# The routing of all blocks at once with the norm on VectorE, and an even attention with spread turns, unit 0 ahead and the head norm's factors in the output weights

## The chip, the cores and the metric

The kernel runs on one core of a Trainium2 chip. The metric is the device time of one execution in microseconds (us). Engines: TensorE (PE, its weight loads PEld), VectorE (DVE), ScalarE (ACT), GpSimd (POOL), SyncE (SP, which issues most DMAs).

## The reference, cut to what matters

Two transformer stages follow each other on 512 tokens of width 1024, all in float32. The second has two layers, an even and an odd one, and each ends in a routed mixture of 32 experts. What the change touches:

```python
# even layer: differential attention, 4 heads of 2 maps; then a norm over each head
a_out = rmsnorm(softmax(q1 k1) v - lam * softmax(q2 k2) v, subln_g) * (1 - lambda_init)
m = concatenate([a_out, latent_attention]) @ w_o       # w_o: 1024 x 1024
# both layers: norm, then the router
x = layer_norm(ALPHA * x + m, ln1_g, ln1_b)
grp = argmax(softmax(x @ w_rg + b_rg))                 # 4 groups of 8 experts
top_v, top_i = top_k(e_logits of that group, 2)
gate = softmax(top_v) * g_w
# experts: each token's two rows, gathered in lists per expert
y = silu(xb @ w1[e]) * (xb @ w3[e]) @ w2[e] * w
```

## The kernel before

A stage is a class whose methods write one instruction list per engine; the order on each engine is the order written out, and engines wait for each other on counting semaphores (`wait_ge`). `then` issues an operation and makes its own engine wait for its end. `wait_end` waits for all that an earlier stage has signalled.

**Products (`Dense`).** A product goes through pieces of 128 rows of a weight matrix. For each piece ACT makes a rounded high part (L692) and DVE the rest (L727, or L729 when the weights are scaled by a gain). PE then multiplies three times for each of four token blocks (L189, the helper `mm`), and DVE or ACT take the accumulators out. `pe_beside(i)`, `act_beside(i)` and `dve_beside(i)` insert other work after piece i.

**`EvenProj`** (38 pieces) makes queries, keys and values of the even layer. Pieces 32 and 33 are followed by the turns of head 0.

**`EvenMix`** has 32 units of 128 query rows: units 0 to 15 are the 4 differential heads (two score maps each), 16 to 31 the 8 latent heads, two at a time. In step n PE turns the weights of unit n-3 (L2436), makes the scores of unit n (L2420 or L189), does one turn of heads where `due` has one (L2400) and multiplies the values of unit n-5 (L2452 or L2457). DVE takes each map's maximum (L2549), the reciprocals of the sums (L2558, L2566), and combines the maps of even units (L2611). POOL combines those of odd units (L2641, L2642) and divides later ones (L2654). ACT does the exponentials (L2506). A turned head goes to PSUM bank 7; ACT takes the high half (L2488), then DVE the low half (L2541, L2544), and only then may PE use the bank for the next. `due` puts k and q of heads 1 to 3 in steps 1, 2, 5, 6, 9 and 10, then the latent heads (mk, mq) in steps 11 to 26 without a gap, and the mixed heads in 28 to 31. Steps 26 and 27 of `dve_norm` multiply the four normed heads by the row factor and by the gain, block by block (L2589, eight operations a step).

**`OutRoute`** (two layers) is the output product, the norm, the router and the lists. In its last four pieces (`pe_blocks`, `dve_blocks`) the work goes block by block: PE finishes a block's sum, DVE adds it to x (L772), takes the statistics (L3123, L3124), ACT the root (L3068), DVE the reciprocal. PE turns the block (L3036) and makes its 36 logits from the raw rows. The norm of block 0 is two DVE operations (L3150, L3145). Blocks 1 to 3 are scaled by ACT (L3074), then POOL multiplies by the gain (L3252) and adds the bias (L3253). Each normed block is written to `xd` and `xa` by SP. Then `route` corrects the logits with the statistics (L3175, L3177, pair by pair for four blocks), finds the group with `top8` over padded values (L3156, L3159, L3161), masks, finds the experts with `top8`, makes one-hots (L3195, their sum L3197), and the gates. `lists` copies the two PE sums from PSUM, adds the prefixes block by block, makes ranks, and builds selectors by eight comparisons (L3230). PE multiplies the selectors with token numbers and gates (L189 on 64 columns), and four operations make the row numbers (L3237 to L3240). POOL gathers the tokens of experts 0 and 1 (L3261). SP loads the weights of expert 1 only after the first gather, those of expert 0 earlier.

**`Experts`** turns the gathered tokens (L3343), splits the weights (L3408, L3463) and multiplies, expert after expert, with the weights streaming in.

## Time and profile before

| | us |
|---|---|
| median of 3 runs | 3568.32 (3567.33 to 3570.15) |
| the profiled execution | 3554.19 |
| its span | 3552.9 |
| even attention | 129.4, from 1744.0 to 1873.4 |
| blocks and routing, first layer | 49.3, from 1911.4 to 1960.7 |
| experts, first layer | 603.2 |

The profile is one execution. PEclk is the granted clock of TensorE as a share of 2.4 GHz. Idle time of an engine is put down to who released it; the chain is followed back from the last instruction.

### The profile page before, as it was taken

The page shows a single profiled execution, that of the slowest core. Times are in us where ns is not written, and L with a number is a line of the kernel's source. Part 1 is how long each engine was busy: PE and PEld are TensorE (multiplying, and loading weights), DVE is VectorE, ACT ScalarE, POOL GpSimd, SP SyncE. Part 2 cuts the span into 40 slices and gives each one's busy share as a digit, 9 for nine tenths or more (in the row PEclk, how much of TensorE's full clock was granted, in tenths as well). Part 3 has the DMA queues.
Part 4 walks back from the last instruction along what each step waited for, and adds up shares of the span by engine and source line. Part 5 has one row for each costly group of instructions (what it writes and reads, how often), then busy time and mean ns, then how long its engine had stood idle before and what let it go on. Part 6 is the DMA issues. An engine that isn't in the chain of part 4 may idle for free. (4 is left out here: it accounts for less than half of the span.)

```text
span 3552.9 us, 42265 instructions
## 1 busy us (share of the span) xinstructions
PE 3270.6 (92%) x16668; PEld 2719.4 (77%) x16669; DVE 2241.1 (63%) x3508; ACT 1801.9 (51%) x2689; POOL 394.9 (11%) x331
## 2 busy tenths in 40 slices
PE   8989899999989999999987999999789879999995
PEld 6789777877878777878766777788667868888874
DVE  5755343435855443333675888899743668988886
ACT  3333342323333342333462778888633628888884
POOL 1101000000101000000141111111100121111110
PEclk9988999999989999999998999999989989999998
DMA  4210122221120122222203899988722238898994
GB/s 139 72 56 1 64 79 95 95 81 63 50 80 1 48 95 75 93 88 89 72 1 110 327 351 364 359 348 353 301 71 103 80 144 336 357 361 356 361 359 178
DMA packets 135163, 590.99 MB, mean 166 GB/s; under 512 B 29616, under 2 KB 35632, under 8 KB 110256
## 3 DMA queue, kind: packets, MB, share of 16 engines
q1 hardware_dynamic: 115664, 569.92, 41.5%
q0 software_dynamic: 19296, 18.30, 2.2%
q8 instruction: 135, 2.21, 0.2%
q14 instruction: 68, 0.56, 0.0%
HBM read 594.40 MB, written 44.04 MB: 180 GB/s over the span
## 5 line engine op out<-in xcount | busy, mean ns | idle before, releaser
L189 PE MATMUL ps<-r,r 128*128 128x512 f32 (+4 forms) x11048 | 2593.7, 393 | 66.8 <-DVE r L2075 23.1
L189 PEld LDWEIGHTS ps<-r,r 128*128 128x128 f32 x11048 | 2046.2, 190 | 536.8 <-issue 63.8
L3463 DVE TENSOR_TENSOR r<-mem,r 128x1024 fp32r<-128x1024 f32 x768 | 902.5, 1220 | 133.6 <-ACT r L3408 127.3
L3408 ACT ACTIVATE r<-mem 128x1024 fp32r<-128x1024 f32 x768 | 788.3, 1061 | 226.5 <-PE ps L189 144.4
L692 ACT ACTIVATE r<-mem 128x512 fp32r<-128x512 f32 (+3 forms) x518 | 338.7, 661 | 906.4 <-PE ps L189 900.0
L727 DVE TENSOR_TENSOR r<-mem,r 128x512 fp32r<-128x512 f32 (+1 forms) x272 | 185.5, 688 | 436.6 <-ACT r L692 435.5
L729 DVE SCALAR_TENSOR_TENSOR r<-mem,r 128x512 fp32r<-128x512 f32 (+3 forms) x246 | 171.7, 714 | 263.6 <-ACT r L692 261.9
L3321 POOL DMA_INDIRECT xa<-mem,memu x64 | 101.5, 1587 | 964.7 <-ACT mem L3433 964.7
L3261 POOL DMA_INDIRECT mem<-xd,memu x64 | 99.2, 1550 | 84.2 <-PE ps L3343 35.1
L1666 PE MATMUL ps<-mem 128*128 128x65 f32 x800 | 99.8, 282 | 0.0
L1666 PEld LDWEIGHTS ps<-mem 128*128 128x128 f32 x800 | 96.7, 199 | 0.0
L1874 DVE RECIPROCAL mem<-ps 128x4 f32<-128x4 f32 x40 | 7.3, 182 | 132.8 <-PE ps L1666 132.7
L1792 ACT ACTIVATE mem<-ps 128x512 f32<-128x512 f32 (+1 forms) x96 | 46.6, 525 | 87.3 <-PE ps L1654 87.0
L3433 ACT ACTIVATE mem<-ps,mem 128x512 f32<-128x512 f32 x128 | 80.7, 686 | 13.0 <-PE ps L189 13.0
L3469 DVE TENSOR_TENSOR r<-ps,r 128x512 fp32r<-128x512 f32 x128 | 82.1, 681 | 4.4 <-ACT r L3413 4.4
L537 PE MATMUL ps<-mem 128*128 128x128 f32 x288 | 44.4, 306 | 43.6 <-DVE mem L3696 19.7
L3343 PEld LDWEIGHTS ps<-mem 128*128 128x128 f32 x512 | 68.1, 192 | 18.0 <-issue 12.9
L3343 PE MATMUL ps<-mem 128*128 128x128 f32 x512 | 69.0, 279 | 12.6 <-DMA mem<-xd,memu 12.6
L3413 ACT ACTIVATE r<-ps 128x512 fp32r<-128x512 f32 x128 | 68.6, 586 | 17.2 <-PE ps L3343 17.2
L537 PEld LDWEIGHTS ps<-mem 128*128 128x128 f32 x288 | 36.7, 157 | 51.7 <-issue 28.2
L189 PE MATMUL ps<-mem 128*128 128x93 f32 (+3 forms) x320 | 50.3, 324 | 25.5 <-DMA mem<-in_nsa_cmp_w 14.7
L1861 DVE TENSOR_REDUCE mem<-ps 128x1 f32<-128x512 f32 (+3 forms) x160 | 67.4, 480 | 6.7 <-PE ps L1624 6.4
(392 smaller groups left out, 2883.2 us busy)
## 6 DMA issues: line engine op xcount, KB each, us to landing
mem<-in_w_up SPq DMA_DIRECT2D x80, 2048.0 KB, 18.5
mem<-in_w_down SPq DMA_DIRECT2D x80, 2048.0 KB, 7.9
mem<-in_w_gate SPq DMA_DIRECT2D x64, 2048.0 KB, 13.2
mem<-in_w_in SPq DMA_DIRECT2D x10, 2048.0 KB, 7.9
mem<-in_odd_w_qkv SPq DMA_DIRECT2D x6, 2048.0 KB, 8.4
mem<-in_w_o SPq DMA_DIRECT2D x4, 2048.0 KB, 10.4
mem<-in_rel SPq DMA_DIRECT2D x16, 512.0 KB, 3.3
mem<-in_even_w_in SPq DMA_DIRECT2D x3, 2048.0 KB, 8.0
```

The lines of the kernel that those rows point to most:

```text
L189: r = e.matmul(out, a, b, start=start and i == 0, stop=stop and i == n - 1, skip_group_check=skip)
L537: r = pe.e.transpose(self.ps(u)[:, k, :], src[:, c:c + 128], self.K.ident)
L692: act.e.activation(wh, w, ACT.Copy, scale=scale).then_inc(*self.S["dn_hi"](self.p0 + i))
L727: r = dve.e.tensor_tensor(wl, w, wh.bitcast(F32), SUB)
L729: r = dve.e.scalar_tensor_tensor(wl, w, job.gain[:, kk:kk + 1], wh.bitcast(F32), MUL, SUB)
L1666: r = pe.e.matmul(self.result(n)[:, 65 * t:65 * t + 65], src[:, c:c + 128], self.F.V[:, j, slot, :], start=j == 0, stop=j == t)
L3261: pool.e.indirect_dma_start(self.XG[e % 2], None, self.K.xd[:, :], bass.IndirectOffsetOnAxis(self.IDX[:, 1, e:e + 1], 0), bounds_check=S - ...
L3321: pool.e.indirect_dma_start(self.K.xa[:, :], bass.IndirectOffsetOnAxis(self.R.IDX[:, 1, e:e + 1], 0), self.YY[e % 2], None, bounds_check=S ...
L3343: r = pe.e.transpose(self.turned(half)[:, k, :], self.XG[e % 2][:, 4 * half + k::8], self.K.ident)
L3408: act.e.activation(wh, w, ACT.Copy).then_inc(*self.S["ex_wh"](self.l, e, i))
L3463: dve.e.tensor_tensor(wl, w, wh.bitcast(F32), SUB).then_inc(*self.S["ex_wl"](self.l, e, i))
L3469: dve.e.tensor_tensor(self.XL[e % 2][:, k, :], self.turned(half), self.XH[e % 2][:, k, :].bitcast(F32), SUB).then_inc(*self.S["ex_xl"](sel ...
```

## The change

In `EvenProj`, unit 0's scores follow piece 35, and its maxima and exponentials follow on DVE and ACT. `EvenMix` starts its loops for these at unit 1. The buffers of E are rotated so that unit 0's lie outside the projection's weight ring. `due` places mk and mq of the eight latent heads in steps 3, 11, 14, 17, 20, 22, 24 and 26 and the ones after them; each head has one of four buffers. The head norm's gain goes into the output weights (`gain=source.M.sg`, four columns of the gain and four of ones), and the norm is one operation a head. In `OutRoute` DVE does the norm of all four blocks (`norm`), ACT and POOL none; the logits are corrected as they come. The group is found by a maximum, a comparison and the smallest index over all blocks. PE adds the rank prefixes in the accumulator; the selectors are two operations and in the single-pass type; POOL makes the values (numbers, and the gates in a high and a low part).

```diff
 class OutRoute
+    def norm(t):
+            x = K.X[:, t, :]
+            dve.wait_ge("rt_p", self.l, "turn", t, 1)
+            dve.then("ln_g", v.scalar_tensor_tensor(x, x, self.nmu[:, t:t + 1], self.gains.gb, ADD, MUL), sid, t)
+            v.scalar_tensor_tensor(x, x, self.mv[:, t, 1:2], self.gains.bb, MUL, ADD).then_inc(*S["ln_b"](sid, t))
...
         for t in range(4):
+            if t:
+                norm(t - 1)
+            if t == 3:
+                self.logits(dve, 0)
...
             job.dves(dve, self, job, t, self.acc(job, t)[:, 0:job.n])
             moments(t)
             roots(t)
+        self.logits(dve, 1)
+        norm(3)
...
-        for t in range(1, 4):
-            x = K.X[:, t, :]
-            pool.wait_ge("ln_a", sid, t)
-            pool.then("ln_g", pool.e.tensor_tensor(x, x, self.gains.gb, MUL), sid, t)
-            pool.then("ln_b", pool.e.tensor_tensor(x, x, self.gains.bb, ADD), sid, t)
+        pool.wait_ge("rt_v", l, "oh")
+        p.tensor_tensor(OV[:, :, :, 0:32], self.oh, bc(self.val.rearrange("p t k -> p k t"), 3, 32), MUL)
+        pool.wait_ge("rt_v", l, "gt")
+        pool.then("rt_g", p.tensor_tensor(self.gates, self.oh, bc(self.gt.rearrange("p t k -> p k t"), 3, 32), MUL))
+        pool.then("rt_g", p.tensor_copy(OV[:, :, :, 32:64], self.gates))
+        p.tensor_tensor(OV[:, :, :, 64:96], self.gates, OV[:, :, :, 32:64].bitcast(F32), SUB).then_inc(*S["rt_g"](l, "values"))
...
 pe_blocks
-                if i == n - 3:
-                    if j >= 1:
-                        self.pe_turn(pe, j - 1)
-                    if j >= 2:
-                        self.pe_logits(pe, j - 2)
+                if i == n - 3 and j >= 1:
+                    self.pe_turn(pe, j - 1)
+                if i == n - 2 and j >= 2:
+                    self.pe_logits(pe, j - 2)
+        self.pe_logits(pe, 2)
         self.pe_turn(pe, 3)
-        self.pe_logits(pe, 2)
         self.pe_logits(pe, 3)
...
 route
+        dve.then("rt_v", v.tensor_reduce(self.gm, groups, AX.X, MAX))
+        v.tensor_tensor(goh, groups, bc(self.gm, 2, 4), ALU.is_equal).then_inc(*S["rt_v"](l, "goh"))
+        v.tensor_tensor(ge, groups, bc(self.gm, 2, 4), SUB).then_inc(*S["rt_v"](l, "ge"))
+        dve.then("rt_v", v.tensor_tensor(goh, goh, bc(self.first, 1, 4), MUL))
+        dve.then("rt_v", v.tensor_reduce(self.mn, goh, AX.X, MIN))
+        dve.then("rt_v", v.tensor_tensor(goh, goh, bc(self.mn, 2, 4), ALU.is_equal))
+        dve.then("rt_v", v.tensor_scalar(goh, goh, 1.0, 1e30, SUB, MUL))
+        dve.then("rt_v", v.tensor_tensor(ml.rearrange("p t (g n) -> p t g n", g=4),
+                                         lg[:, :, 4:36].rearrange("p t (g n) -> p t g n", g=4), bc(goh, 3, 8), ADD))
...
+        dve.then("rt_v", v.tensor_tensor(oh, bc(bc(ei, 1, 4), 1, 2), bc(which, 3, 32), ALU.is_equal), l, "oh")
...
 lists
+        dve.then("rt_v", v.tensor_tensor(self.ranked, self.oh, bc(ranks, 1, 2), MUL))
+        dve.then("rt_v", v.tensor_reduce(self.rv.rearrange("p t k -> p k t"), self.ranked, AX.X, ADD))
         for k in range(2):
-            for t in range(4):
-                r = v.tensor_scalar(self.OS[:, k, t, :], self.iota, self.rv[:, t, k:k + 1], None, ALU.is_equal)
+            v.tensor_tensor(self.OS[:, k], bc(self.iota, 1, 4), bc(self.rv[:, :, k], 2, 128),
+                            ALU.is_equal).then_inc(*S["rt_v"](l, "os", k))
...
+        dve.then("rt_v", v.tensor_scalar(self.ixf, bank[1][:, 0:32], NONE, None, ADD))
+        v.tensor_copy(self.IDX[:, 1, :], self.ixf).then_inc(*S["rt_v"](l, "rows"))
...
 pe
+        pe.e.matmul(bank[:, 0:128], self.ustr, ohs, start=True, stop=False, skip_group_check=True)
+        for t in range(3):
+            o = bank[:, 32 * t + 32:128].rearrange("p (t n) -> p t n", n=32)
+            r = pe.e.matmul(o, self.ones, bc(ohs[:, 32 * t:32 * t + 32], 1, 3 - t), start=False, stop=t == 2,
+                            skip_group_check=True)
...
+        pe.wait_ge("rt_g", l, "values")
+        for k in range(2):
+            pe.wait_ge("rt_v", l, "os", k)
+            for t in range(4):
+                r = pe.e.matmul(K.bank[1][:, 0:96], self.OS[:, k, t, :], self.OV[:, k, t, :], start=k == 0 and t == 0,
+                                stop=k == 1 and t == 3)
...
 EvenProj
+        if i == 35:
+            self.mix.pe_scores(pe, 0)
...
+        if i == 36:
+            for m in range(2):
+                self.mix.act_exponentials(act, 0, m)
...
 EvenMix
-        for h in range(8):
+        for h, n in enumerate((3, 11, 14, 17, 20, 22, 24, 26)):
             for i, what in enumerate(("mk", "mq")):
-                self.due[11 + 2 * h + i] = (what, h)
+                self.due[n + i] = (what, h)
...
 dve_norm
-                for t in range(4):
-                    x = M.MIX[:, t, 128 * h:128 * h + 128]
-                    r = v.scalar_tensor_tensor(x, x, M.var[:, 4 * h + t:4 * h + t + 1], M.sg, MUL, MUL)
+                x = M.MIX[:, :, 128 * h:128 * h + 128]
+                v.tensor_tensor(x, x, bc(M.var[:, 4 * h:4 * h + 4], 2, 128), MUL).then_inc(*S["em_v"](sid, "mixed", h))
```

## Rows read from the trace of the kernel before

**Rows 1.** The page: lines of the chain that ended last, shares of the span.
```profile
PE ps L189 31%; DMA mem<-in_w_up 5%; PE ps L3343 1%; DMA mem<-in_w_gate 1%; ACT r L3408 1%; DVE r L3463 1%; PE ps L3384 1%; PE ps L2436 0%; DVE mem L2549 0%; DVE mem L3177 0%; ACT mem L3433 0%; DVE r L2863 0%; DVE r L2685 0%; PE ps L2457 0%; DMA xa<-mem,memu 0%
```
**Rows 2.** By stretch: us; PE, PEld, DVE, ACT, POOL busy (count); PEclk, DMA share, GB/s.
```profile
1744.00:1873.40 129.40, 111.11 (x842) 83.26 (x842) 91.72 (x193) 84.69 (x199) 55.07 (x52) 0.99 0.00 1
1764.00:1769.20 5.20, 5.20 (x35) 3.33 (x34) 3.78 (x9) 4.42 (x11) 1.95 (x3) 1.00 0.00 0
1775.40:1808.90 33.50, 28.66 (x193) 21.68 (x193) 22.81 (x47) 24.00 (x59) 16.09 (x16) 1.00 0.00 1
1911.40:1927.50 16.10, 15.32 (x100) 13.26 (x99) 10.12 (x26) 4.66 (x10) 2.56 (x2) 1.00 0.45 183
1927.50:1960.70 33.20, 8.52 (x54) 8.04 (x52) 27.14 (x95) 9.03 (x12) 15.38 (x7) 0.55 0.27 105
1960.70:2563.90 603.20, 589.75 (x2688) 479.63 (x2688) 521.00 (x508) 480.80 (x573) 95.15 (x62) 0.99 0.89 350
2888.00:2919.80 31.80, 7.87 (x51) 7.41 (x50) 26.67 (x93) 9.03 (x12) 14.90 (x7) 0.58 0.26 101
```
**Rows 3.** Timeline, blocks to experts: start, us, engine, line, operation [idle before it, releaser].
```profile
1913.86 1.28 DVE L3150 SCALAR_TENSOR_TENSOR mem<-mem 128x1024 f32<-128x1024 f32 x1
1915.10 0.69 DVE L772 SCALAR_TENSOR_TENSOR mem<-mem,ps 128x512 f32<-128x512 f32 x1
...
1925.98 0.69 DVE L772 SCALAR_TENSOR_TENSOR mem<-mem,ps 128x512 f32<-128x512 f32 x1 [2.97 <-PE ps L189]
...
1955.68 1.91 POOL L3261 DMA_INDIRECT mem<-xd,memu  x1 [15.73 <-DVE mem L3242]
...
1960.68 1.94 PE L3343 MATMUL ps<-mem 128*128 128x128 f32 x8 [6.81 <-DMA mem<-xd,memu]
```
**Rows 4.** DVE and POOL behind the blocks (first: one line's ns min/median/max).
```profile
L3177 DVE SCALAR_TENSOR_TENSOR mem<-mem x8: 255/2220/2373, 1929.9 to 2895.5; 128x36 f32<-128x36 f32 x8
...
1930.30 2.36 POOL L3252 TENSOR_TENSOR mem<-mem 128x1024 f32<-128x1024 f32 x1 [0.63 <-ACT mem L3074]
...
1930.34 2.37 DVE L3177 SCALAR_TENSOR_TENSOR mem<-mem 128x36 f32<-128x36 f32 x1
...
1938.87 1.11 DVE L3161 CAST mem<-memu 128x32 f32<-128x32 uint32 x1
```
**Rows 5.** Chain of waits in the routing: start, us, engine and line.
```profile
1942.30 0.76 DVE memu L3159 x5
...
1943.82 0.29 DVE r L3197
...
1948.49 1.67 DVE mem L3230 x8
1950.20 3.69 PE ps L189 x16
1953.91 0.20 DVE mem L3237
```
**Rows 6.** A line of POOL with 256 columns: ns min/median/max, first and last start.
```profile
L2000 POOL TENSOR_TENSOR mem<-mem x24: 717/732/742, 253.3 to 1187.8; 128x256 f32<-128x256 f32 x24
```
**Rows 7.** Timeline of the even attention, as rows 3.
```profile
1752.68 1.04 POOL L2641 TENSOR_TENSOR mem<-mem 128x512 f32<-128x512 f32 x1 [58.49 <-DVE mem L2559]
...
1784.71 0.64 PE L2400 MATMUL ps<-mem 128*96 128x128 f32 x4 [1.28 <-DVE r L2544]
...
1841.22 2.19 DVE L2589 SCALAR_TENSOR_TENSOR mem<-mem 128x128 f32<-128x128 f32 x8
...
1845.18 3.00 DVE L2589 SCALAR_TENSOR_TENSOR mem<-mem 128x128 f32<-128x128 f32 x8
...
1845.41 1.04 PE L2436 MATMUL ps<-mem 128*128 128x128 f32 x4 [3.04 <-DVE mem L2608]
...
1846.11 2.91 PE L189 MATMUL ps<-r,r 96*128 96x512 f32 x6
...
1851.26 1.63 PE L189 MATMUL ps<-r,r 96*128 96x512 f32 x6
```

More of the change, by code:

```diff
@@ L2299, in dve_beside @@
             v.tensor_copy(M.heads[0][1], K.bank[0][:, :]).then_inc(*S["em_lo"]("even_mix", "k", 0))
+        if i == 36:
+            for m in range(2):
+                self.mix.dve_maximum(dve, m)
     def pool(self, pool):
```

202 lines of the change are left out of this document (79 added, 123 removed).

## The prediction

> **What bounds the kernel now.** I read the page first. The chain that ended last runs mostly through the matmuls of TensorE (PE), with the weight stream of the experts behind it [rows 1]. So a microsecond counts only where PE waits. The busy times by stretch show where that is in the parts the change touches [rows 2]. The two passes over all 64 experts are PE and the weight stream side by side (589.8 of 603.2 us busy in the first). The attention of the even layer, 129.4 us, has PE busy for 111.1, so 18.3 us of it are waits. The blocks of the output product are full (15.3 of 16.1). What comes behind them is not: in 33.2 us of routing PE works 8.5 at a granted clock of 0.55, close to the lower of its two levels (1.2 of 2.4 GHz), while VectorE (DVE) is busy for 27.1. The second layer repeats that: 7.9 of 31.8. Both layers' routing is therefore a serial DVE chain with nothing of size beside it, and whatever leaves that chain leaves the time.
>
> **Routing, step by step (first layer; the second has the same rows 960.2 us later).** Before, the last block's accumulation starts on DVE at 1925.98, the gather is issued at 1955.68 and the first transposes of the experts start at 1960.68 [rows 3]. Six terms:
>
> (a) *Norm on DVE, from the last block to the logits.* Before, POOL multiplies and adds the gains of blocks 1 to 3 in six operations of 2.36 us. DVE's small operations of that stretch take as long as POOL's do: the logits operation of 128x36 takes 0.26 us at the least and 2.22 in the median of its eight, one of them beside POOL's from 1930.3 to its end at 1932.7, and a cast of 128x32 takes 1.11 [rows 4]. The change takes POOL out and gives DVE two passes of 1.28 us per block [rows 3]. I walked this through. Norm 0 now stands ahead of block 1's addition, which started at 1915.10 and now starts at 1916.4. PE's turn of block 1 waits 0.8 us for it. Norm 1 (2.6 us) ends as block 2's product does, which the wait and a postponed product have moved to 1921.3. Norm 2 ends as block 3's does, at about 1926.8, and logits 0 (0.46) are in front of block 3's addition, so it starts at 1926.9 instead of 1925.98. The statistics and the root then take the 2.3 us of before (the root is back by 1929.2), logits 1 0.5, norm 3 2.6, logits 2 and 3 0.9: logits complete at 1933.2. Before, they were complete at 1937.55, one end of POOL's after another (1932.7 and two times 2.4). Gain 4.4 us, of which PE's turn and logits of block 3 (about 1932.7) leave only half a microsecond unused. Bounds 3.1 (one more pass shows in front of an addition) and 5.3 (the shift of the last addition is avoided).
>
> (b) *Logits to the one-hots' sum.* Before 1937.58 to 1944.11, 6.5 us, of which POOL's last operation lengthened the cast by 0.9 [rows 4, 5]. After: two small reductions and five elementwise steps at 0.21, the masked add 0.32, eight values 0.5, their search 0.76, cast 0.22, both one-hots in one operation of 256 columns 0.46 (between the 0.29 of 128 and the 0.69 of 512), sum 0.29: 4.0 with the extra "ge" step [rows 3, 5]. (0.21 is the 0.20 of a small dependent step, rounded up.) Gain 2.5.
>
> (c) *Ranks.* Before, from 1944.11 to the ranks, just ahead of 1948.49, DVE copies PSUM, adds prefixes in six steps and multiplies and reduces twice, 4.35 us [rows 5]. After, PE adds the prefixes: four small matmuls at 0.3 each, 1.2 (the lists' sixteen ran at 0.23 [rows 5]), then one product (0.46) and one reduction (0.45), 2.2 with a wait. Gain 2.1. Bounds 1.4 (the matmuls at twice 0.23 and a hand-over) and 2.6.
>
> (d) *Lists' selectors.* Eight operations in 1.66 us become two of 128x512 at 0.69 (the size of the additions in [rows 3]), 1.35. But four POOL operations are new beside them: a 128x256 product takes POOL 0.73 us [rows 6], the last three wait for the gates, and [rows 4] show DVE held until POOL's end. I add two of them, 1.5 us. Loss 1.2, between a loss of 2.6 (all four) and a gain of 0.3 (none).
>
> (e) *Lists' matmuls.* Before, 16 instructions in 3.67 us, all behind the last selector [rows 5]. After, there are 8, four of which run while DVE builds the second half: four at 0.23 and a start, 1.0. Gain 2.7. Bounds 1.8 (all eight come behind the last selector) and 3.0.
>
> (f) *Indices.* Four dependent steps of 0.2 [rows 5] become two, gain 0.4. The gather's own 4.9 us and the 0.9 us in front of it stay.
>
> Sum 10.9 us a layer, 21.8 for two. Behind it nothing new is late: the token blocks for the gather leave DVE at 1932.4, so their writes are out by the time the gather wants them, about 1944.8; ScalarE and DVE split the first four weight pieces while the tokens are on their way, and both move together. The weights of expert 1 and later are issued after the first gather, so the stream starts earlier by the same amount.
>
> The skill bears on (d). The Trainium skill, "SBUF — State Buffer", section "Who interferes with whom", says that an operation of VectorE with two SBUF inputs and a GpSimd operation that reads SBUF exclude each other for a whole instruction. By this rule the trace agrees, 2.22 us against 0.26 on one form, and it speaks against the new POOL operations. Without the exclusion the layer's sum would be 12.4; with all four blocking, 10.9 less 1.4, that is 9.5.
>
> **The even attention.** Unit 0's scores, maxima and exponentials move into the projection, behind piece 35. They cost PE 1.1 us there, a unit's scores (a unit without a turn takes 2.6 with them), so the projection ends that much later; the copies that end it stay. DVE no longer has two maxima in front of its first sums. The first POOL combine, 1752.68 before, I place at 1751.9 [rows 7]: gain 0.8. Bounds 0 and 1.9.
>
> Turns: a unit that has a turn with a low half took 3.7 us from unit 11 to 19 (33.5 us for nine, PE busy 28.7), because DVE waits for ScalarE's high half, which waits for both exponentials; PE's wait of 1.28 us for DVE ahead of a turn is this alternation [rows 2, 7]. A unit without one takes 2.6 (two in 5.2, PE full). Three such units (13, 16, 19) lose their turn: -3.3. Units 3 and 4 gain one, +2.2 if they pay in full, and unit 27 gains one, +0.6. Net gain 0.5. Bounds: a loss of 2.8 (nothing comes back at 13, 16 and 19) and a gain of 3.3.
>
> Norm: 16 operations of 128x128, in two groups of 2.19 and 3.00 us, become four of 128x512 at 0.69, 1.4 a group [rows 7]. The first group stands on the chain: PE waits 3.04 us behind it, and then runs at its lower level (six matmuls 2.91 us, 1.63 five microseconds later). I take 0.9 for the first group and 1.3 for the second with part of the clock. Gain 2.2. Bounds 0.9 and 4.
>
> The part that the factors play in the output weights (ScalarE scales by a column, DVE's low part is a three-operand form) costs nothing: those pieces lie under the product, PE-bound; without that cover it would be 16 times 0.03.
>
> Sum 3.5. All: 21.8 + 3.5 = 25.3 us. The profiled execution took 3554.19 (span 3552.9), so it would take 3528.9; the median of the runs shown is 14.1 higher, and I take the same difference off it: **3543.0**.
>
> **Rivals.** A measurement of this kernel can tell about 0.2%, 7 us, from no change.
>
> *POOL's values set the lists* (0.13). Place: the wait "values" ahead of the lists' matmuls. POOL's three last steps start with the gates (about 1939.4) and take 0.73 each at least; a broadcast operand may cost more (the nearest other row is 1.04 for 512 columns). If DVE's two selectors also stand between them, values come 2 to 3 us behind my 1942.8. For it: [rows 4, 6]. Against: two of these four overlap DVE work that reads PSUM. Price 3 a layer: 3549.
>
> *The attention gives more* (0.12). PE waits 18.3 us there; if spreading breaks the ScalarE-DVE alternation also in the units that keep a turn, 8 more go: 3535. *It gives nothing* (0.12): units 3, 4 and 27 pay for their turns in full and nothing comes back: 0.8 and 2.2 won, 2.8 lost, 3546, and up to 3549 if the hoisted unit gains nothing either.
>
> *PE falls to its lower clock in the blocks* (0.02): the end on the other side. Place: turns 1 and 2 among the blocks, which now wait for DVE's additions behind the norms. The only fall in the attention followed a wait of 3.04 us [rows 7]; I forecast 0.8, and it decides only if waits of that length come up. Then the 15.3 us of PE work there [rows 2] double, in both layers: 30.6 lost against 25.3 won, 3573.6, above before by 5.3. *The weight stream eats the gain* (0.03): if the experts ran behind the stream instead of PE, an earlier start would be given back; the chain has 6% of the span on these transfers, which speaks for it, and 31% on the matmuls, which speaks against [rows 1]. 3560 or more; which side of the 0.2% it ends on is open.
>
> *The change does less than it says* (0.03): if the two STT passes of the norms were held up by something I do not see, (a) falls away: 3552.
>
> The forecast has 0.55. The range 3529 to 3557 takes in both attention cases, the POOL case, and the bounds of (a), (c), (d) and (e), one or two of them at a time in both layers (all at their ends would be 10 us a side for the two layers, which I don't expect together). Faster by over 0.2%: 0.94; within 0.2%: 0.04; slower by over 0.2%: 0.02.
>
> **What would show it.** Right: no DVE operation of 36 columns over 0.3 us; the logits complete 6.3 us behind the last block's addition; lists in some 2 us or less after the last selector; last addition to first expert transpose near 23 us instead of 34.7; PE busy in the blocks unchanged at clock 1.00; the attention near 126 us with PE waits fallen at the norms. Wrong: PE held by "values", a selector over 1 us, a fall of the clock before the last block, or more than 3 us a unit at units 3 and 4 that is not regained at 13, 16 and 19. The forecast is wrong as a whole if the stretch from the last addition to the experts shrinks by less than 8 us a layer, or if it does shrink and the experts take longer by as much.

## The result, and the profile after

The changed kernel took 3533.35 us (median of 4, from 3524.18 to 3538.93) against 3567.82 (4 runs, 3567.23 to 3570.15): ratio 0.9911, interval 0.9892 to 0.993, so 25 to 39 us faster. The forecast was 3543.0 with a range of 3529 to 3557. The profiled execution took 3524.18 us (span 3522.9), 30.0 less than the profiled one of before. A second series of both kernels, below, gave 0.9907 (0.9883 to 0.9931).

The changed kernel by stretch (us; busy us and count of PE, PEld, DVE, ACT, POOL; granted clock, DMA share, GB/s), in the order of [rows 2]: the even attention, the output product's blocks, the routing, the first experts, and the second layer's routing.

```profile
1744.45:1872.40 127.95, 111.35 (x843) 83.32 (x842) 87.74 (x179) 83.40 (x195) 54.93 (x52) 0.99 0.00 1
1910.40:1927.50 17.10, 16.48 (x111) 14.49 (x110) 15.53 (x29) 3.53 (x9) 0.00 (x0) 1.00 0.66 265
1927.50:1948.00 20.50, 6.17 (x37) 5.45 (x36) 17.61 (x56) 6.89 (x10) 5.82 (x6) 0.59 0.26 96
1948.00:2547.20 599.20, 587.90 (x2688) 480.12 (x2688) 520.87 (x508) 480.82 (x573) 95.95 (x62) 0.99 0.89 352
2870.70:2891.40 20.70, 6.95 (x45) 6.24 (x44) 18.10 (x58) 6.89 (x10) 6.67 (x6) 0.64 0.24 94
```

The reader is to see that the gain is in the third and fifth lines: 33.2 us of routing have become 20.5 and 31.8 have become 20.7, on the same engine as before (DVE is busy for 17.6 of 20.5). The blocks kept their clock of 1.00 with DVE now busy 15.5 of 17.1 us. The attention gained only 1.4 us.

Timeline of the changed kernel from the third block to the experts (start, us, engine, line, operation [idle before it, releaser]), which answers [rows 3], and its logits line (ns min/median/max), which answers [rows 4].

```profile
1922.72 1.28 DVE L3153 SCALAR_TENSOR_TENSOR mem<-mem 128x1024 f32<-128x1024 f32 x1
1924.04 1.28 DVE L3154 SCALAR_TENSOR_TENSOR mem<-mem 128x1024 f32<-128x1024 f32 x1
...
1925.82 0.69 DVE L773 SCALAR_TENSOR_TENSOR mem<-mem,ps 128x512 f32<-128x512 f32 x1
...
1931.85 0.26 DVE L3176 SCALAR_TENSOR_TENSOR mem<-mem 128x36 f32<-128x36 f32 x1
...
1935.67 0.29 DVE L3212 TENSOR_TENSOR r<-mem 128x128 fp32r<-128x128 f32 x1
...
1938.39 2.02 DVE L3230 TENSOR_TENSOR r<-mem 128x512 fp32r<-128x512 f32 x2
...
1948.02 1.94 PE L3343 MATMUL ps<-mem 128*128 128x128 f32 x8 [6.15 <-DMA mem<-xd,memu]
```
```profile
L3176 DVE SCALAR_TENSOR_TENSOR mem<-mem x8: 255/256/257, 1925.5 to 2875.9; 128x36 f32<-128x36 f32 x8
```

Last addition to the experts' first transposes: 22.2 us instead of 34.7. The logits are complete 6.3 us behind the last addition (1925.82 to 1932.11). The second pass of the logits takes 0.26 us all eight times, where its median was 2.22.

The chain of waits behind the gates, changed kernel (start, us, what):

```profile
1937.66 0.63 POOL mem L3251
...
1938.34 0.40 POOL r L3252
...
1938.82 1.06 POOL r L3253
...
1939.92 1.96 PE ps L3073 x8
...
1943.18 4.71 DMA mem<-xd,memu
```

Here one thing is not as forecast: POOL's gate values are on the chain, and the eight list matmuls (L3073) start behind them. Two of the forecast's signs of being wrong have come up with it, the wait for "values" and a selector over 1 us (the two of a layer take 0.89 and 1.21 us).

### The profile page after: what moved, and what is told of

It is laid out like the page before. It is cut to its first block, busy times and chain, and to the rows that moved or that the text cites. A ratio compares the mean times of both kernels' runs of the same rounds, so it can differ in the third digit from the quotient of the medians.

```text
span 3522.9 us, 42167 instructions
## 1 busy us (share of the span) xinstructions
PE 3264.1 (93%) x16658; PEld 2713.3 (77%) x16659; DVE 2231.0 (63%) x3430; ACT 1797.1 (51%) x2683; POOL 372.3 (11%) x327
## 4 chain that ended last, share of the span: by engine, by line
PE 35%; DMA 6%; DVE 5%; ACT 3%; issue 1%; SPq 0%; POOL 0%; DVEq 0%; ACTq 0%; POOLq 0%
PE ps L190 31%; DMA mem<-in_w_up 5%; PE ps L3343 1%; ACT r L3408 1%; DVE r L3463 1%; PE ps L3384 1%; PE ps L2446 0%; DMA mem<-in_w_gate 0%; DVE mem L2562 0%; ACT mem L3433 0%; DVE r L2874 0%; DVE r L2696 0%; ACT mem L2505 0%; DVE mem L2891 0%; ACT r L2841 0%
## 5 line engine op out<-in xcount | busy, mean ns | idle before, releaser
L728 DVE TENSOR_TENSOR r<-mem,r 128x512 fp32r<-128x512 f32 (+1 forms) x256 | 174.8, 688 | 421.5 <-ACT r L693 420.1
L730 DVE SCALAR_TENSOR_TENSOR r<-mem,r 128x512 fp32r<-128x512 f32 (+3 forms) x262 | 183.4, 716 | 279.5 <-ACT r L693 277.9
L1652 PE MATMUL ps<-r,r 128*128 128x512 f32 (+3 forms) x160 | 65.6, 410 | 4.2 <-ACT r L1780 4.1
## 6 DMA issues: line engine op xcount, KB each, us to landing
mem<-in_w_o SPq DMA_DIRECT2D x4, 2048.0 KB, 10.6
```

The costliest lines, as they stand in the source:

```text
L728: r = dve.e.tensor_tensor(wl, w, wh.bitcast(F32), SUB)
L730: r = dve.e.scalar_tensor_tensor(wl, w, job.gain[:, kk:kk + 1], wh.bitcast(F32), MUL, SUB)
```

## Reading every run by the same marks

The timed runs of one kernel lie up to 26 us apart, more than most of the steps in question. So beside its time every experiment is read by marks in its trace that it shares with the others: A, the first transposes of line 2222 in the even projection; B, the first transposes of block 0 in the output product (line 3048 of the changed kernel, 3036 before); C, the rank matmul (3061; before 3048); D, the first gather (3261); E, the experts' first transposes (3343). B to E come once a layer. Then come the first layer's experts up to the next layer's first transposes (line 538), and the second layer's up to the end. These are starts taken from the timelines of the profiled executions, in us, the two layers side by side.

```
kernel        A        A-B      B-C            C-D            D-E          experts
before        1729.12  183.51   31.54  31.55   11.51  11.45   5.00  3.99   618.6  633.1
after         1729.57  182.08   24.36  24.37    7.17   7.12   4.84  4.37   614.7  631.4
after_again   1740.21  182.16   24.36  24.38    7.16   7.11   4.44  4.41   619.0  633.4
r_only        1740.19  183.51   24.99  24.38    7.17   7.41   4.91  4.14   616.7  633.1
e_only        1746.33  180.80   32.79  32.81   11.53  11.48   5.25  3.97   618.2  631.6
norm_dve      1744.42  183.54   26.63  26.63   11.47  11.47   5.21  4.07   617.2  629.8
delay         1736.52  182.08   34.44  35.77    7.16   7.12   5.27  4.28   617.9  633.9
pool_beside   1733.88  182.11   33.38  32.54    7.22   7.19   4.56  4.42   616.9  631.0
best          1743.14  180.34   24.50  24.39    6.62   6.57   4.91  3.44   617.7  635.1
split_only    1734.83  182.12   24.36  24.76    6.81   6.77   4.51  3.40   616.5  632.1
due_old       1744.17  180.66   24.81  24.38    7.16   7.13   4.80  4.46   617.5  634.1
norm_old      1738.64  182.53   24.37  25.58    7.16   7.12   4.79  4.37   617.9  633.0
no_hoist      1741.56  182.42   24.37  25.67    7.17   7.41   4.56  4.16   617.8  633.6
no_root       1737.38  178.34   24.37  24.38    7.15   7.12   4.59  4.47   615.5  632.2
```

Before against after: 1.4 us from A to B, 7.2 in each layer from B to C, 4.3 in each from C to D. Together 1.4 + 2 x 11.5 = 24.4 us.

Two of the marks depend on the granted clock of PE as well as on the edit, and this has to be taken off before two kernels are compared.

*From A to B.* After PE's wait at the norm of the even layer the clock fell to 0.5 for some 3.4 us in ten of the fourteen traces (in the changed kernel from 1845.67 to 1849.08), and did not fall in e_only, due_old, best and no_root. The changed kernel and e_only have the same attention, and PE's wait there is 1.70 us in both:

```profile
1844.19 0.63 PE L2446 MATMUL ps<-mem 128*128 128x128 f32 x4 [1.70 <-DVE mem L2619]
1844.57 2.50 PE L190 MATMUL ps<-r,r 96*128 96x512 f32 x6
```
```profile
1860.93 0.63 PE L2445 MATMUL ps<-mem 128*128 128x128 f32 x4 [1.70 <-DVE mem L2618]
1861.31 1.91 PE L189 MATMUL ps<-r,r 96*128 96x512 f32 x6
```

The first pair is the changed kernel, with the fall, the second e_only, without it. The fall costs 1.3 us from A to B (182.1 against 180.8). So the four kernels without it are compared with e_only, and the others with the changed kernel.

*From B to C.* The clock also falls around the end of the last block, ahead of PE's long waits in the routing. In the traces with the changed kernel's routing (pool_beside aside), where it fell 19.4 us or more behind B, the logits' last matmuls were through or nearly so, and B-C is 24.4 us. Where it fell 17.6 to 18.8 us behind B, they ran slower: this is the case in all values of B-C that stand 0.1 to 1.4 us above what their edits explain (24.50, 24.76, 24.81, 24.99, 25.58, 25.67, and 35.77 of delay's second layer). In norm_old's second layer the sixteen last logits matmuls took 3.53 us, and 1.98 in the changed kernel.

## Experiments

**1. The changed kernel again** (after_again: no edit).

> The changed kernel once more, beside the kernel before on this chip. Theory A (the terms stand, the rest is the experts' weight stream, whose length varies from run to run): the ledger of the two traces gives 1.0 us in the even attention and 11.7 us in each layer's routing, 24.4 together, and the stretch from the first expert's transposes to the last scatter-add, 603.2 and 602.9 us before, comes out between 599 and 604 us; 24 to 32 us faster than before by the medians. Theory B (the change itself shortens the expert stage, because its loads start in another order): both expert stretches are under 600 us again and the time is 33 to 36 us under before.

Measured: 3538.52 us (6 runs, 3526.69 to 3545.39) against 3568.62 for before (19 runs, 3554.15 to 3577.87), 30 us less by the medians. The marks between A and D repeat the first trace within 0.1 us. The expert stretches are 619.0 and 633.4, and from the first transposes to the last scatter-add, the measure of the expectation, 603.7 and 603.8: theory A, the change does not shorten them. But A itself comes at 1740.21, 10.6 us later than in the first trace, and up to A the two runs execute the same instructions. This was not in either theory. By stretch, from the start to A (before, after, e_only):

```profile
0.00:1729.12 1729.12, 1616.95 (x8493) 1367.95 (x8495) 844.93 (x1652) 590.61 (x1053) 90.97 (x106) 0.96 0.21 73
```
```profile
0.00:1729.57 1729.57, 1617.01 (x8492) 1366.37 (x8494) 844.83 (x1654) 590.83 (x1053) 90.97 (x106) 0.96 0.21 73
```
```profile
0.00:1746.33 1746.33, 1635.85 (x8493) 1387.20 (x8494) 845.69 (x1654) 590.87 (x1053) 90.77 (x106) 0.95 0.21 72
```

The same 8493 matmul instructions are busy for 1617 us or for 1636, while DVE, ACT and POOL agree within 1 us. The difference lies in stretches where PE falls to its lower clock in one execution and less in another: up to A it stood at its lower level for 150 us in before, 147 in the changed kernel, 178 in after_again and 184 in e_only. One of them, 25 us of before and 28 us of e_only that hold nearly the same work (178 and 167 matmuls):

```profile
1070.00:1095.00 25.00, 24.10 (x178) 23.10 (x177) 10.33 (x30) 5.70 (x12) 0.74 (x1) 0.92 0.00 1
```
```profile
1080.00:1108.00 28.00, 27.56 (x167) 26.56 (x166) 10.37 (x30) 5.80 (x12) 0.74 (x1) 0.74 0.00 1
```

Over the fourteen traces A lies between 1729.12 and 1746.33, and the middle one of the thirteen others is 1740.2: the profiled execution of before was the luckiest of all up to there, and that of the changed kernel the next.

**2. The routing part alone** (r_only: the diff's parts for the output product's last stage and the routing, on the kernel before; the even layer as before).

> The kernel before with the routing part of the change alone (norm of the blocks on VectorE, logits per block, one-hots and lists of all blocks at once); the even attention is untouched. Theory A: the traces of before and after give 11.7 us a layer, and the attention of before keeps its 1.0, so 23 to 31 us faster than before, with last addition to first expert transposes at 22.2 us instead of 34.7. Rival (part of the gain in the blocks belonged to the even attention or to the factors in the output weights): the same stretch stays above 24 us in the first layer, and the time is under 20 us better.

Measured: 3541.27 us, ratio 0.9924 (0.9904 to 0.9944). A-B is 183.51, as before to the hundredth. B-C and C-D are those of the changed kernel, but for 0.6 us in B-C of the first layer (the clock) and 0.3 in C-D of the second (not looked into). So theory A: the routing's gain is its own, 22 us by the marks, and 27 by the medians.

**3. The even layer's part alone** (e_only: unit 0 in the projection, the turns' due times, the norm's products, the factors in the output weights).

> The kernel before with the even layer's part alone (unit 0 in the projection, turns spread, norm as two products, factors in the output weights). Theory A, from the two traces: the output product starts 1.0 to 1.4 us earlier and the time is 1 to 2 us better, under half of the forecast's 3.5. Rival 1, the forecast: 3.5 us. Rival 2 (the extra gain of the changed kernel lies here, by a phase shift of what follows): 8 us or more, though the attention shows 1.

Measured: 3568.3 us (12 runs), ratio 0.9993 (0.9979 to 1.0008). A-B is 2.7 us shorter than before, of which 1.3 are the fall of the clock that did not come; the other 1.4 are theory A's, and less than the forecast. No 8 us are hidden here, which strikes rival 2. And yet the time did not move, because the routing, whose code is that of before, took 1.25 us longer in each layer. The timelines name the instruction. Kernel before, second layer:

```profile
2897.74 2.38 POOL L3253 TENSOR_TENSOR mem<-mem 128x1024 f32<-128x1024 f32 x1
2897.74 0.17 DVE L3179 COPY mem<-mem 128x16 f32<-128x16 f32 x1
```

The even part alone, the same pair:

```profile
2912.72 2.34 POOL L3263 TENSOR_TENSOR mem<-mem 128x1024 f32<-128x1024 f32 x1
2912.73 2.36 DVE L3189 COPY mem<-mem 128x16 f32<-128x16 f32 x1
```

DVE's copy and POOL's last addition start within 0.01 us of each other, the copy 4 to 5 ns behind POOL in both layers of before and 8 to 9 ns behind in both layers of e_only. In the first the copy gets through (0.17 us), and it is the cast after it that is held (1.11 us [rows 4]). In the second the copy is held to POOL's end. The Trainium skill, "SBUF — State Buffer", section "Who interferes with whom", says that whichever of the two issues first keeps the other out for its whole instruction. The traces agree as far as the one that is held is held to the other's end; who issued first they can't show, since POOL's start stands first in both. The forecast took the profiled 1.11 us for the price; it was the better side of a tie. The change removes the tie with POOL's products.

**4. The norm step alone** (norm_dve).

```diff
-            pool.then("ln_g", pool.e.tensor_tensor(x, x, self.gains.gb, MUL), sid, t)
-            pool.then("ln_b", pool.e.tensor_tensor(x, x, self.gains.bb, ADD), sid, t)
...
+            dve.then("ln_g", v.scalar_tensor_tensor(x, x, self.nmu[:, t:t + 1], self.gains.gb, ADD, MUL), sid, t)
+            v.scalar_tensor_tensor(x, x, self.mv[:, t, 1:2], self.gains.bb, MUL, ADD).then_inc(*S["ln_b"](sid, t))
```

> The kernel before with one step of the routing part alone: the norm of all four blocks as two instructions each on VectorE, and POOL's six 128x1024 products and ScalarE's norm taken away; logits, top values, ranks and lists as before. The forecast's term (a): last block's addition to logits complete 4.4 us shorter a layer, bounds 3.1 to 5.3, so 8.8 us of the time; the VectorE instructions on 128x36 fall from up to 2.4 us to 0.3. Rival: the gain needs the logits taken inside the blocks (the last block's product waits for norms that are now in VectorE's order), and the step alone gives 2 us a layer or less, as the third block's two norms (2.6 us) stand ahead of the logits.

Measured: B-C 26.63 in both layers instead of 31.54, 4.9 us a layer; forecast 4.4. The rival's 2 us are out. The logits' second pass, kernel with the norm step alone:

```profile
L3174 DVE SCALAR_TENSOR_TENSOR mem<-mem x8: 256/256/257, 1947.3 to 2904.8; 128x36 f32<-128x36 f32 x8
```

So the one step that takes POOL's products away, though DVE gets two passes a block more for them, gives 9.8 of the 24.4 us. By the medians it is 15.0 (3553.6, ratio 0.9951, interval 0.993 to 0.9973).

**5. POOL put back beside the blocks** (pool_beside: the changed kernel with six unused products).

```diff
...
+        for t in range(1, 4):
+            pool.wait_ge("ln_v", self.name, t, "nmu")
+            for i in range(2):
+                pool.then("rt_j", p.tensor_tensor(junk, hm, hm, MUL), l, t, i)
```

> The changed kernel with six unused 128x1024 products put back on POOL where the kernel before had its norm: two behind each of the last three blocks' means. No engine waits for their results (only ScalarE's exponential of the gates' chain stands behind them, so that they are over before the pools' own work). Theory (VectorE's small instructions were long because POOL worked beside them): the logits' instructions on 128x36 grow from 0.25 us to 1 us or more, VectorE's norms of 128x1024 grow too, and the stretch to the rank matmul gets 1.5 to 5 us longer a layer, though VectorE does the same work. Rival (they were long for the row dependence on the logits and on the norm's own waits): they stay at 0.25 us and the stretch stays at 206.5 and 317.3 us within 0.5.

Measured: 3557.34 us (10 runs) against 3538.52 for the changed kernel in its own series (10.0 and 30.1 us under the before of each series), B-C 33.38 and 32.54 instead of 24.36: 9.0 and 8.2 us a layer. That is more than the 1.5 to 5 expected, and the place is another. Kernel with POOL beside (the two norm lines, ns min/median/max; one pass; PE's turn of block 2):

```profile
L3154 DVE SCALAR_TENSOR_TENSOR mem<-mem x8: 1272/2330/2715, 1917.2 to 2896.8; 128x1024 f32<-128x1024 f32 x8
```
```profile
L3155 DVE SCALAR_TENSOR_TENSOR mem<-mem x8: 1284/2796/2798, 1918.5 to 2898.1; 128x1024 f32<-128x1024 f32 x8
```
```profile
1924.68 2.80 DVE L3155 SCALAR_TENSOR_TENSOR mem<-mem 128x1024 f32<-128x1024 f32 x1
...
1928.13 1.44 PE L3048 MATMUL ps<-mem 128*128 128x128 f32 x8 [2.05 <-DVE mem L773]
```

The logits' passes stayed at 0.26 us but for one a layer of 1.40, since POOL was done by then. The norms' passes went from 1.28 to 2.3 and 2.8 us (medians), the additions behind them came late, and PE waited 2.05 us. In the first layer DVE's held instructions alone add 7.7 us by their rows (five passes of the norms and one of the logits, less 1.28 and 0.26 each); part of the rest is PE's clock, which fell while the blocks still ran, 12.7 and 21.5 us behind B in the two layers. The cause is the theory's (POOL beside DVE), its victim was misplaced.

**6. The routing longer by ten microseconds** (delay: eight unused products on DVE).

```diff
...
+        for i in range(8):
+            dve.then("rt_v", v.tensor_tensor(junk, hm, hm, MUL))
```

> The changed kernel with eight unused 128x1024 products on VectorE in the routing of each layer, between the indices of the top values and the one-hots (such a product takes 1.2 to 1.3 us in the traces, so some 10 us a layer). It tests what a microsecond of the routing chain is worth. Theory A (nothing in the experts' weight stream hides it or adds to it): the stretch from the even attention's turn in the projection to the rank matmul grows by 10 us in each layer, the two expert stretches keep their 614 to 619 and 630 to 634 us, and the time goes up by 20 us against the changed kernel. Theory B (the stream sets the end of the experts, and a later start is made up): the expert stretches get 3 us or more shorter. Theory C (an earlier start lets the stream run better, so a later one costs more than itself): they get longer, by 3 us or more, and the time goes up by 26 us.

```profile
1942.16 10.04 DVE L3212 TENSOR_TENSOR mem<-mem 128x1024 f32<-128x1024 f32 x8
```

Measured: 10.1 and 11.4 us more from B to C (1.3 of the second are the clock), expert stretches 617.9 and 633.9, and 3557.54 us (10 runs), 19 above the changed kernel's other series, or 20 when each is counted from the before of its own series. Theory A: a microsecond of the routing chain is worth a microsecond, and the experts neither give back nor add.

**7. The lists in two groups, and the norm's products spread** (best), with **8. the groups alone** (split_only). The edit of the first is

```diff
+        pool.wait_ge("rt_v", l, "os", 1)
...
-        pe.wait_ge("rt_g", l, "values")
+        pe.wait_ge("rt_g", l, "numbers")
...
+        pe.wait_ge("rt_g", l, "values")
...
-        if n in (26, 27):
-            for h in (2 * n - 52, 2 * n - 51):
+        if 26 <= n <= 29:
+            h = n - 26
```

and the second leaves out the first and the last of these.

> The changed kernel with two edits that its trace asks for. (1) The lists' matmuls in two groups: the numbers' eight first, which wait for POOL's first product alone, and the gates' eight into another bank behind them; POOL's three gate instructions start only after the second selector. (2) The even norm's four products one to a turn, in turns 26 to 29, instead of two and two in turns 26 and 27. Theory: the two selectors take 1.35 us together instead of 2.02, as no POOL instruction runs beside them, the numbers' matmuls start with them and not with POOL's last value, and the rank matmul to first expert transposes stretch goes from 12.0 and 11.5 us to 10.5 to 11.0 in both layers; (2) takes 0.6 us of the 1.70 us wait of TensorE at the second norm turn and may keep its clock: 0.5 to 1.5 us. Sum 2.5 to 4 us under the changed kernel. Rival: the indices are not what the gather waits for (its own start of 0.9 us after them stays, and the gates' later products put POOL's queue late), so (1) gives nothing or loses 1 us; and a shift of (2) only moves the wait to the next turns.

> The changed kernel with the lists' matmuls in two groups (numbers first, gates behind them in another bank), but with POOL's gate products where they were, beside VectorE's selectors. It parts two effects of the combined kernel, which had 0.5 us less from the rank matmul to the first gather in each layer: waiting for POOL's values, and POOL beside the selectors. Theory A (both count): the selectors take 2.0 us together again, the numbers' matmuls end with them, and rank matmul to gather is 0.1 us to 0.4 us shorter than the changed kernel's 7.1. Theory B (only the order on TensorE counts): 0.5 us shorter or more, as in the combined kernel. Theory C (the wait for POOL's values cost nothing, since the second selector ended no earlier): no difference.

Timeline of best, then of split_only, at the selectors:

```profile
1950.37 1.29 DVE L3236 TENSOR_TENSOR r<-mem 128x512 fp32r<-128x512 f32 x2
...
1951.21 1.86 PE L3073 MATMUL ps<-r,r 128*128 128x32 f32 x8 [1.89 <-DVE r L3236]
```
```profile
1943.70 2.02 DVE L3236 TENSOR_TENSOR r<-mem 128x512 fp32r<-128x512 f32 x2
...
1944.73 2.08 PE L3073 MATMUL ps<-r,r 128*128 128x32 f32 x8 [2.09 <-DVE r L3236]
```

Without POOL beside them the two selectors take 1.29 us, with it 2.02. C-D is 7.17 in the changed kernel, 6.81 with the groups alone, 6.62 with both: the wait for POOL's values costs 0.36 us and POOL beside the selectors 0.19 more. For split_only that is its theory A. For best it is half of what was expected. Of the 0.73 us that the selectors get shorter, 0.32 come back on PE (its eight list matmuls take 1.9 us and now end 1.41 us behind the last selector, where they ended 1.09 behind it) and 0.22 in the cast of the indices, which takes 0.40 us beside POOL's gates instead of 0.18. In the second layer D-E is 3.4 instead of 4.4 us in both kernels; why the first gather is quicker there was not looked into. A-B is 180.34, 1.7 us less, but the clock did not fall in this trace; against e_only, where it didn't either, the spread norm gave 0.5 us (PE's wait 1.10 instead of 1.70). Whether the spread also keeps the clock up is not shown by one trace. Measured as a whole best took 3542.96 us (6 runs), not below the 3538.52 of the changed kernel's other series; against the before of its own series it has 24.4 us, where the changed kernel had 30.1. The 1.1 us of the lists and the 0.5 of the norm, and the 1.0 of the second layer's gather if it belongs to the edit, are less than the runs can tell. It is the version I would keep, on the marks alone.

**9. The old due times** (due_old).

```diff
-        for h, n in enumerate((3, 11, 14, 17, 20, 22, 24, 26)):
+        for h, n in enumerate((11, 13, 15, 17, 19, 21, 23, 25)):
```

> The changed kernel with the latent heads' turns due where they were, two together from turn 11 on. Theory, the forecast's term: 0.5 us more in the attention as a whole, units 3 to 6 some 2.2 us earlier than in the changed kernel and units 13 to 21 giving back 2.7 us. Rival (spreading is worth nothing here, since the engine that ends each unit is the same): the output product starts within 0.2 us of the changed kernel's, counted from the projection's turn.

Measured (one execution, 3543.38 us), counted from A and against after_again: 2.1 us ahead at unit 6, 0.5 to 0.6 behind from unit 16 to unit 21, 0.3 to 0.4 behind at units 22 to 25, and 1.5 ahead from unit 26 on. Of this turnabout of 1.8 us 1.3 are the clock, which did not fall here. Counted against e_only, where it didn't either, the old due times are 0.2 us ahead at B. What takes the gain of the new due times back is the turn that they put into unit 27, across PE's wait at the norm: the three matmuls with the turned head's low half wait another 0.44 us for DVE there (rows of experiment 11), and due_old, with no turn in that unit, has no such wait. So it is the rival that holds: spread turns are worth nothing by the end, -0.2 us against the +0.5 of the forecast.

**10. The old form of the norm** (norm_old) and **11. no square root** (no_root), both on the changed kernel, one execution each.

```diff
...
+                for t in range(4):
+                    x = M.MIX[:, t, 128 * h:128 * h + 128]
+                    r = v.tensor_scalar(x, x, M.var[:, 4 * h + t:4 * h + t + 1], None, MUL)
```
```diff
...
-                act.e.activation(M.var, M.var, ACT.Sqrt).then_inc(*S["em_a"](sid, "root"))
...
-            dve.wait_ge("em_a", sid, "root")
```

> The changed kernel with the even norm as sixteen instructions of 128x128, one a head and block, instead of four products of 128x512. Forecast's term: 2.2 us in all, from 0.9 in the first group of the norm, and 1.3 in the second with the clock. The trace of the routing part alone, which has the norm of before, had a wait of 3.04 us where the changed kernel has 1.70, and about the same loss of clock behind it (1.7 against 2.0 us). So theory A: the wait is 3.0 us, the output product starts 1.0 to 1.6 us later than the changed kernel's counted from the projection's turn. Rival, the forecast: 2.2 us or more later.

> The changed kernel without the square root in the even layer's head norm (the norm then divides by the mean square and not by its root, so this part of the computation is left out), and so without ScalarE's two function tables of 1.28 us each around it. It asks what holds TensorE for 1.70 us at the second norm turn. Theory A (the tables: ScalarE's copy for the latent head's turn came 2.6 us late, VectorE stood behind it with the norm's products): the wait falls under 0.7 us, the granted clock stays at its upper level through the following products (six of 128x512 in 1.6 us, not 2.4 to 2.5), and the output product starts 2.5 to 4 us earlier, counted from the projection's turn. Theory B (VectorE's own load: copies, maxima and two products of 1.28 us a turn): the wait stays at 1.2 us or more, and 1 us or less is won.

PE behind the norm's first group: the wait, and the six matmuls that follow it. Routing part alone (the norm of before), norm_old, due_old, no_root; the changed kernel and e_only stand above.

```profile
1856.48 0.92 PE L2437 MATMUL ps<-mem 128*128 128x128 f32 x4 [3.04 <-DVE mem L2609]
```
```profile
1853.67 0.63 PE L2446 MATMUL ps<-mem 128*128 128x128 f32 x4 [2.07 <-DVE mem L2621]
1854.06 2.44 PE L190 MATMUL ps<-r,r 96*128 96x512 f32 x6
```
```profile
1859.15 0.63 PE L2446 MATMUL ps<-mem 128*128 128x128 f32 x4 [2.15 <-DVE mem L2619]
1859.53 1.64 PE L190 MATMUL ps<-r,r 96*128 96x512 f32 x6
```
```profile
1849.49 0.63 PE L2446 MATMUL ps<-mem 128*128 128x128 f32 x4 [1.10 <-DVE mem L2615]
1849.87 1.91 PE L190 MATMUL ps<-r,r 96*128 96x512 f32 x6
```

In the changed kernel, norm_old, e_only and no_root a second wait is hidden inside the time of the six matmuls: the weights of the last three are the low half that DVE has still to make. In no_root:

```profile
1850.81 0.53 PEld L190 LDWEIGHTS ps<-r,r 96*128 96x128 f32 x3 [0.44 <-DVE r L2554]
```

So six matmuls in 1.91 us are not a lower clock. The clock did not fall in no_root, and in the changed kernel, where it fell, they take 2.50.

The sixteen instructions cost only 0.4 us more than the four products (wait 2.07 against 1.70, A-B 182.53 against 182.12, the clock fallen in both); both theories had asked for 1 us or more. Eight of them took 1.66 us here, against 2.19 for the first group of before [rows 7], where each also reads the 128-column tile of factors. Of the 0.97 us by which the wait falls from 3.04 to 2.07, 0.53 go with that operand, and the rest with the turn of unit 27, which keeps PE busy into the wait (due_old, without it, waits 2.15 where the changed kernel waits 1.70). In all the new norm gives 1.3 us of the 1.4 from A to B: the hoist has 0.3 (next) and the turns -0.2.

Leaving out the root gives 3.7 us against the changed kernel (A-B 178.34), of which 1.3 are the clock; against e_only it is 2.5, as long as the two tables (2 x 1.28), and PE waits 1.10 us. Theory A had asked for three things: the start of the output product came earlier as it said, the clock stayed up as it said, and the wait stayed above its 0.7 us, so DVE's own load keeps a part, as theory B has it. Since the clock also stayed up in e_only with the root in place, this trace does not show that the tables bring it down. The tables in the changed kernel's timeline:

```profile
1833.70 1.28 ACT L2535 ACT_TABLE_LOAD   x1
...
1836.55 1.28 ACT L2505 ACT_TABLE_LOAD   x1 [0.85 <-PE ps L2446]
```

**12. No hoist** (no_hoist: unit 0's scores, maxima and exponentials back in the attention).

> The changed kernel with the first unit's scores, maxima and exponentials back in the attention and not in the projection. The forecast gave the hoist 0.8 us, the two traces 0.45. Theory: unit 3 starts 0.4 to 0.8 us later than in the changed kernel, counted from the projection's turn, and the output product too. Rival: the first units are held by ScalarE's exponentials anyway, and nothing is left of it by unit 5.

Measured (one execution, 3543.5 us): A-B 182.42 against 182.1, the clock fallen in both: 0.3 us. Unit 3 starts 0.4 us later. It is there, at the lower end of what was expected. The other single executions took 3539.62 (norm_old), 3530.3 (no_root) and 3531.68 us (split_only).

## Why the prediction was right, and where it was not

**Routing, 10.9 us a layer forecast, 11.5 measured.** Counted from the start of the output product (1873.26 before, 1872.28 after), the logits are complete after 64.3 and 59.8 us. The terms from the two profiled executions:

```
                         forecast   measured
(a) norm to logits          4.4       4.5    (64.3 - 59.8)
(b) one-hots' sum           2.5       2.7    (6.56 -> 3.85)
(c) ranks                   2.1       1.9    (4.32 -> 2.38, C to the selectors)
(d) selectors              -1.2      -0.4    (1.66 -> 2.02)
(e) lists' matmuls          2.7       2.3    (3.7 -> 1.45 behind the last selector)
(f) indices                 0.4       0.5    (1.78 -> 1.32, with the gather's start)
```

(a) came as it was walked through: the last addition moved back by 0.8 us relative to the product (forecast 0.9), PE's turn waited 0.62 us (0.8), and the clock in the blocks stayed at 1.00. (b) is a little better, and in other executions of the kernel before it would be better by 1.25 more, by the tie of experiment 3. In (d) I charged two POOL operations of the four, 1.5 us. They cost 0.7 (2.02 us for the selectors against 1.29 in best). But (e) is smaller for the same POOL operations: the matmuls waited for the last value (1939.87) and not for the selectors alone. So the first rival was half true. POOL's values do set when the lists start, at 0.36 us a layer and not 3, since the gates were ready at 1937.6 and not at 1939.4. The sign "a selector over 1 us" did not fit the sum: with 1.5 us added to 1.35 the forecast itself had two selectors of 1.4 us.

**Even attention, 3.5 us forecast, 1.4 measured.** All three terms gave less than forecast, with the clock fallen in both traces:

```
                         forecast   measured
unit 0 ahead                0.8       0.3    (no_hoist)
turns                       0.5      -0.2    (due_old against e_only)
norm                        2.2       1.3    (the rest of 1.4)
```

In the turns, the first units cost 2.2 us (forecast 2.2), and by unit 16 2.8 had come back (forecast 3.3); another 0.2 went by unit 23, and the turn of unit 27 cost 0.5 (forecast 0.6). In the norm the step that failed is this: "I take 0.9 for the first group and 1.3 for the second with part of the clock". The first group gave its 0.9 (2.19 us to 1.29) and PE's wait fell by 1.3 us (3.04 to 1.70), but the clock fell all the same, and with the low half of unit 27 behind the wait the second 1.3 shrank to 0.4. In e_only the clock did stay up, and A-B was 2.7 us shorter. I had read the wait as DVE's norm instructions; no_root shows that ScalarE's tables around the root stand in front of them. The forecast's rival of an attention that gives nothing (0.12) was nearer to what happened. Its price was added up wrongly: 0.8 and 2.2 won and 2.8 lost make 3546, and without the 0.8 it is 3547, not 3549. The four bounds (a), (c), (d) and (e) also make 8.6 us on one side and 6.4 on the other for two layers, not 10 on each.

**The sum.** 24.4 us by the marks against 25.3: that they lie so near is partly luck, since two errors of opposite sign are in it, 1.2 us too little in the routing and 2.1 too much in the attention. The experts behind kept their time, and delay shows that they pass a change on one for one.

**The level.** The forecast took 25.3 off the profiled time and added the 14.1 us by which the median of before stood above it. By the medians the gain is 34.5 in the first series and 30.1 in the second, and the ten times of the changed kernel have a median of 3535.9, which is 7 below 3543. Two things are shown in this gap. The profiled execution of before reached A earlier than any other trace, 11 us ahead of the middle, so most of the 14.1 is likely the clock upstream and no property of the change. (The other traces up to A are of other kernels with the same matmuls; no second one of before was taken.) And both intervals reach down to 25 us. What stays open is whether the remaining 6 to 10 us are chance. The traces hold nothing outside the marks that would make it up. Most other kernels lean the same way: against before, norm_dve has 15.0 us by the medians and 9.8 by the marks, r_only 27 and 22, delay 10 and 3, pool_beside 10 and 7, and e_only, the only one that keeps POOL's norm in the routing, 0.3 and 0.2. But best leans the other way, with 24 by the medians and 27 by the marks, so chance is not out. If the timed runs of before mostly lost the tie of experiment 3, as e_only did, 2.5 us of it would be explained; that wasn't tried.

## What to carry to other kernels

Before the length of a small instruction is taken as its cost, look at what the other engines do in the same instant: six POOL operations off the path of VectorE gave 9.8 of 24.4 us though VectorE got more to do. Where single runs scatter by more than the step, compare marks inside the traces around the edit, and look at the granted clock between them: here they repeated within 0.1 us where the clock was the same, and moved by up to 1.3 where it wasn't, while the totals moved by 20. A single trace of an edit can win or lose that much by the clock alone. When a wait shrinks, check whether what it cost afterwards (here the lower clock) goes too, and look one engine further back for what the late instruction waited for.

## What the hardware did that I had not expected

- PE's lower clock after a wait did not follow from the wait's length. It came behind 3.04, 2.07 and 1.70 us, and did not come behind 2.15 us (due_old), behind 1.10 us (best, no_root), nor behind the same 1.70 us in e_only, where the instructions are those of the changed kernel. Identical matmuls up to A were busy for 1617 or 1636 us by such falls.
- Two 128x1024 streams of DVE and POOL slow each other (pool_beside): DVE's passes went from 1.28 to 2.8 us, and POOL's from 1.90 to 2.75 when they began under one of DVE's. In before even a product of 128x1 took 1.40 us beside POOL, where the same line takes 0.16 alone.
- A 128x16 copy takes 0.17 or 2.36 us beside the same POOL instruction, when its start moves by 4 ns.
